# A causal depthwise convolution inside a hybrid decoder layer: 15 of its 62 tap operations move from VectorE to GpSimd

## The chip, the cores and the metric

One core of a Trainium2 chip. The metric is the device time of one launch in microseconds (us), the median of several executions. PE is TensorE (PEld its weight loads), DVE is VectorE, ACT is ScalarE, POOL is GpSimd, SP is SyncE, which here only issues DMAs.

## The reference, cut to what matters

One decoder layer for 512 prompt rows and 8 sample rows, width 1024. After one combined projection `z = x @ w_in`, four head groups work side by side (a convolution module, two kinds of sparse attention, a pooling mixer), then comes an output projection, a layer norm, a feed-forward block (1024 to 4096 to 1024) and a second layer norm. The change concerns the convolution module alone:

```python
def conv_module(u, buf, dw, dw_b, ln_g, ln_b, pw):
    a, g = jnp.split(u, 2, axis=-1)
    z = a * jax.nn.sigmoid(g)
    zc = jnp.concatenate([buf, z], axis=1)
    y = lax.conv_general_dilated(zc, dw[:, None, :], ...feature_group_count=C_CONV) + dw_b
    y = jax.nn.silu(layer_norm(y, ln_g, ln_b))
    return y @ pw, zc[:, -(CONV_W - 1):]
```

256 channels, each with a filter of 31 taps of its own over the rows before it, float32 throughout.

## The kernel before, in words

Channels lie on the 128 partitions and rows in the free dimension, so 256 convolution channels are two channel tiles, t = 0 and t = 1. One tap of one tile is one operation on 128 x 512 elements: `yc[t] += zc[t, k:k+512] * w[t, k]`, with the weight read from a column of `vec`. There are 31 x 2 = 62 of them, listed in `TAPS` in the order (k=0,t=0), (k=0,t=1), (k=1,t=0) and so on. All run on DVE (line 1299 for the two with k = 0, line 1302 for the other 60). Each waits on the semaphore `vtap` until the operation before the previous one has finished, since only that one wrote the same tile.

The program is written as one list of steps, `TL`, made by `timeline()`; each engine walks through this list and issues, in this order and in a queue of its own, what it has to do at each step. Nothing is reordered at run time, so a wait on an engine holds up everything behind it on that engine.

The first part of the list goes over the 18 panels of `w_in` (numbered 0 to 17; a panel is 1024 x 128 weights). For panel i:

- `load_panel`: SP loads it into one of three buffers `raw`.
- `split`: float32 products are made from three passes over rounded parts. ACT writes the rounded weights `wH` (line 941), DVE the rest `wL = raw - wH` (line 1240). `split i+1` stands ahead of `mm i` in the list.
- `mm`: PE runs 48 matmuls (line 597) and waits before them for `l_done`, the semaphore of `wL`.
- `evac`: ACT copies the sum out of PSUM into `zT`.

Between the panels other steps are strung, one stage of each per panel: `nsa b` for the eight sample sequences (PE: compression matmuls of line 606 and selection scores of line 623; DVE: lines 1258, 1264, 1268 and 1272, and at `kv` line 1275; ACT: lines 972 to 978), the `qn` copies (DVE, lines 1282 and 1283), and the convolution:

- after panel 4, `glu` (DVE, lines 1290 to 1293) writes `zc` and counts `glu_done` to 2;
- after each of the panels 4 to 9 a `taps` step, with 6, 6, 13, 13, 12 and 12 tap operations. In the list a `taps` step stands ahead of the `split` of the next panel but one: the taps after panel 7 stand ahead of `split 9`, which `mm 9` waits for;
- at the end of the last `taps` step the eight sample rows (lines 1307 to 1309) and `conv_done`;
- after panel 10 `cmean` (PE, line 750, waits for `conv_done`; DVE subtracts the mean, line 1354), later `cvar` and `cpw`, the norm and the pointwise product.

POOL has little to do: seven memsets at the start (line 1152), then `pdiff 0` after panel 8 and `pdiff 1` after panel 10 (running sums for the pooling mixer, lines 1164 to 1189, on the buffers `pa` and `pb`; `pdiff 0` waits for the last pooling panel, number 8, and its result is read by the PE step `pool 0`, line 738, after `cmean`, and waited for by SP ahead of the output of `pool_sample`), then one scaling per attention unit (line 1195), the residual of the first layer norm (line 1199) and a square per panel of the up projection (line 1204).

Of the kernel before, what the change touches and what calls it, by code (L numbers as in the profile page):

```python
# [8 lines left out]
ALU = mybir.AluOpType  # L9
# [7 lines left out]
T, B = 512, 8  # L17
# [9 lines left out]
CW = 31  # L27
# [48 lines left out]
PAD = ("pad", 0)  # L76
PADS = (0, 0, 0, 0, 0)
PER_PANEL = 7
TAPS = [(k, t) for k in range(CW) for t in range(2)]


def timeline():

    tl = [("load_x", 0), ("load_panel", 1), ("load_small", 0), ("load_panel", 2), ("load_w1", 0)]
    tl += [("split", 0)]
    tl += [("xsplit", k) for k in range(KT)]

    def panel(i, mid=()):
        out = []

        if i + 1 < N_PANELS and i + 1 != OUT0:
            out.append(("split", i + 1))
        if i + NRAW < N_PANELS and (i >= OUT0 or i + NRAW < OUT0):
            out.append(("load_panel", i + NRAW))
        out.append(("mm", i))
        out += list(mid)
        out.append(("evac", i))
        return out

    def spread(first, n, extras):  # L100

        out = []
        for q in range(n):
            out.append(("att", first + q))
            out += [s for s in extras[q * len(extras) // n:(q + 1) * len(extras) // n] if s != PAD]
        return out

    def pieces(i, first, n, extras):

        out = [s for s in panel(i) if s[0] not in ("mm", "evac")]  # L110
        q = 0
        for s in spread(first, n, extras):
            if s[0] == "att":
                out.append(("mm", i, q, n))
                q += 1
            out.append(s)
        return out + [("evac", i)]

    nt = 2 * CW
    taps = [0, nt // 10, nt // 5, nt // 5 + 13, nt // 5 + 26, nt // 5 + 38, nt]  # L120
    pending = []
    att = 0
    M = lambda lo, hi: [s for u in range(lo, hi) for s in (("mu", u), ("mp", u - 1))]
    extras = {15: M(1, 2) + [("ctr", 0), ("zrow", 0)] + M(2, 3) + [("cimp", 0)],
              16: M(3, 4) + [("zrow", 1)] + M(4, 7),
              17: M(7, 11)}
    for i in range(N_IN_PANELS):
        b = i - NSA_PANEL
        if i >= ATT_PANEL:
            tl += pieces(i, att, PER_PANEL, extras[i])  # L130
            att += PER_PANEL
        else:
            tl += panel(i, pending)
        pending = []
        if i == 1:
            tl.append(("load_nsa", 0))
        if i == 2:
            tl.append(("load_state", 0))
            tl.append(("cmpp", 0))
            pending = [("kv", 0)]  # L140
        if i == NSA_PANEL:
            tl.append(("qn", 0))
        if 0 <= b < B:
            tl.append(("nsa", b))
            pending = [("kv", b + 1)]
            if b < B - 1:
                tl.append(("load_nsa", b + 1))
        if b == B - 1:
            tl.append(("load_post", 0))
        if i == 4:  # L150
            tl.append(("glu", 0))
        if 4 <= i < 10:
            tl.append(("taps", (taps[i - 4], taps[i - 3])))
        if i == 8:
            tl += [("out_early", 0), ("pdiff", 0)]
        if i == 10:
            tl += [("cmean", 0), ("pool", 0), ("pdiff", 1), ("qm", 0), ("out_conv", 0)]
        if i == 11:
            tl += [("cvar", 0)]
        if i == 12:  # L160
            tl += [("cpw", 0), ("pool", 1), ("load_lo", 0)]
        if i == 14:
            tl += [("csc", 0), ("zcols", 0), ("win", 0), ("mu", 0)]
    tl += [("out_z", 0)]
    side = [("zrow", 2), ("own", 0), ("vrow", 0), ("vrow", 1), ("msplit", 0), ("msplit", 1), ("msplit", 2), ("msplit", 3)]
    for u in range(11, MU + 1):
        side += [("mu", u), ("selv", u - 11), ("mp", u - 1)]
    side += [("selv", k) for k in range(MU + 1 - 11, 4 * (B - 1))]
    side += [("stat", k) for k in range(3)] + [PAD] * PADS[0] + [("comb", 0)] + [PAD] * PADS[1] + [("comb", 1)] + [PAD] * PADS[2] + [("back", 0)] + [PAD] * PADS[3]
    for b in range(B + 1):  # L170
        side += [PAD] * PADS[4] + [("spv", b)] + ([("load_panel", OUT0 + b - 1)] if 1 <= b <= NRAW else [])
    side += [("split", OUT0), ("mpv", 0), ("fin", 0)]
    tl += spread(att, NU + LAG - att, side)
    tl += [("load_x", 1)]
    tl += [("msplit", q) for q in range(4, KT)]

    for i in range(OUT0, FF0):
        tl += panel(i, [("mean", 0, i - OUT0 - 1)] if i > OUT0 else [])
    tl += [("mean", 0, KT - 1), ("ln", 0)]
    for i in range(FF0, N_PANELS):  # L180
        k = i - (N_PANELS - KT)
        tl += panel(i, [("mean", 1, k - 1)] if k > 0 else [])
    tl += [("mean", 1, KT - 1), ("ln", 1)]
    return tl


TL = timeline()
# [51 lines left out]
def nth(bank, step):  # L239

    return USES[bank].index(step)


def build(nc, a, o):
    ctx = ExitStack()
    with ctx:
        def sem(name):
            return ctx.enter_context(nc.semaphore(name))
# [141 lines left out]
        h_done, l_done, mm_done = sem("h_done"), sem("l_done"), sem("mm_done")  # L390
        acc_read = [sem("acc_read_by_scalar"), sem("acc_read_by_vector")]
        const_done = sem("const_done")
        vch, ach, pch, vtap, vln = sem("vector_chain"), sem("scalar_chain"), sem("gpsimd_chain"), sem("tap_done"), sem("ln_scaled")
        bias_in = sem("bias_in")
        xc_done, cmp_mm, cmp_t1, cmp_u, cmp_th, hid_done, kv_mm, kc_done = (
# [745 lines left out]
        def _(pool):  # L1141
# [10 lines left out]
                nc.gpsimd.memset(buf, value).then_inc(const_done, 1)  # L1152
            up_no = 0
            for kind, n, *part in TL:
                if kind == "pdiff":

                    read(pool, ("mm", PANEL_SLOT.index(S_PO + 1)))
                    tt, copy = nc.gpsimd.tensor_tensor, nc.gpsimd.tensor_copy
                    x = zT[:, S_PO + n, :]
                    if n == 0:  # L1160
                        pool.wait_ge(small_in, 32)
                        pool.wait_ge(state_in, 32)
                        for t in range(2):
                            copy(sp[:, t, :, 15], zT[:, S_PO + t, T:NT])
                    else:
                        pool.wait_ge(pool_mm, 1)

                    def double(dst, src, w):
                        copy(dst[:, 0:w], src[:, 0:w])
                        chain(tt(dst[:, w:T], src[:, w:T], src[:, 0:T - w], ALU.add))  # L1170

                    double(pa, x, 1)
                    double(pb, pa, 2)
                    if n == 1:
                        double(pa, pb, 4)
                        double(pb, pa, 8)
                    w0, w1_ = ((2, 4), (8, 16))[n]

                    for lo, s in ((0, pa), (HD, pb)):
                        q = slice(lo, lo + HD)  # L1180
                        tt(pb[q, 0:16], s[q, 0:16], cst[q, C_INVC + 16 * n:C_INVC + 16 * n + 16], ALU.mult)
                        chain(nc.gpsimd.tensor_scalar(pb[q, 16:T], s[q, 16:T], cst[q, C_INVW + n:C_INVW + n + 1], None, ALU.mult))
                    for lo, w in ((0, w0), (HD, w1_)):
                        rows = slice(lo, lo + HD)
                        chain(copy(pb[rows, T:NT], sp[rows, n, :, 15]))
                        for k in range(1, w):
                            chain(tt(pb[rows, T:NT], pb[rows, T:NT], sp[rows, n, :, 15 - k], ALU.add))
                    chain(nc.gpsimd.tensor_scalar(pb[:, T:NT], pb[:, T:NT], cst[:, C_INVW + n:C_INVW + n + 1], None, ALU.mult))
                    tt(pb[:, :], pb[:, :], x, ALU.subtract).then_inc(pool_d, 1)
# [19 lines left out]
        def _(dve):  # L1209
# [22 lines left out]
            for step in TL:  # L1232
# [62 lines left out]
                elif kind == "taps":  # L1295
                    for k, t in TAPS[n[0]:n[1]]:
                        w = vec[:, V_DW + t * CW + k:V_DW + t * CW + k + 1]
                        if k == 0:
                            ts(yc[:, t, 0:T], zc[:, t, 0:T], w, vec[:, V_DWB + t:V_DWB + t + 1], ALU.mult, ALU.add).then_inc(vtap, 1)
                        else:  # L1300
                            dve.wait_ge(vtap, taps - 1)
                            stt(yc[:, t, 0:T], zc[:, t, k:k + T], w, yc[:, t, 0:T], ALU.mult, ALU.add).then_inc(vtap, 1)
                        taps += 1
                    if n[1] == len(TAPS):
                        tmp = Vn[:, 0, :, :].rearrange("p a b -> p (a b)")[:, 0:B * CW].rearrange("p (b k) -> p b k", b=B)
                        for t in range(2):
# [438 lines left out]
```

## Time and profile before

| | us |
|---|---|
| median of 3 runs | 944.61 (940.42 to 953.58) |
| the profiled execution, its own time | 934.16 |
| its span, first to last instruction | 932.4 |
| busy in the span: PE, DVE, ACT, POOL | 846.1, 435.2, 281.9, 143.9 |

The profile is one execution. Its span is what the rows below are measured in; 1.8 us lie around it. The stretch that the change touches runs from 43.5 us (`glu`) to about 115 us (`cmean`), one tenth of the span.

### The profile page before, as it was taken

The numbers are of one execution on the slowest core, as the hardware profiler recorded it, in microseconds if no ns is written. First come the engines' busy times: TensorE is split into PE (matmuls) and PEld (weight loads), VectorE is DVE, ScalarE is ACT, GpSimd is POOL, SyncE is SP. The second block draws the span as 40 slices with busy tenths as digits, with TensorE's granted clock in tenths as the row PEclk, the third lists the DMA queues.
The fourth block names the chain that finished last, engine by engine and source line by source line (L and its number), as shares of the span: only waits on it lengthen the run. The fifth ranks groups of instructions, "written<-read, shape, count | busy, mean of one in ns | idle before, by whom it ended". The sixth has DMA issues, their size and how long they took to land.

```text
span 932.4 us, 17901 instructions
## 1 busy us (share of the span) xinstructions
PE 846.1 (91%) x6901; PEld 733.2 (79%) x6901; DVE 435.2 (47%) x961; ACT 281.9 (30%) x610; POOL 143.9 (15%) x171
## 2 busy tenths in 40 slices
PE   6999899599899988689899499999999999999993
PEld 6988688466545554378798499999999999999992
DVE  3389953466655675541424633333333333333325
ACT  4222243243422343221312433331133113311104
POOL 0005350022221333111000611110011001100000
PEclk9999999799765899789999699999999999999997
DMA  9455743545646785112333023333323332233202
GB/s 324 132 161 157 191 137 114 204 136 182 211 152 182 225 256 146 32 46 90 96 90 137 1 91 91 91 91 92 94 87 91 101 97 77 94 108 91 68 1 92
DMA packets 73295, 113.26 MB, mean 121 GB/s; under 512 B 25177, under 2 KB 42202, under 8 KB 72538
## 3 DMA queue, kind: packets, MB, share of 16 engines
q1 hardware_dynamic: 65146, 110.28, 38.0%
q10 hardware_dynamic: 8064, 1.84, 0.9%
q8 instruction: 55, 0.90, 0.4%
q14 instruction: 30, 0.25, 0.1%
HBM read 107.66 MB, written 6.52 MB: 122 GB/s over the span
## 4 chain that ended last, share of the span: by engine, by line
PE 54%; DVE 3%; POOL 2%; ACT 1%; ACTq 1%; issue 1%; DVEq 0%
PE psum L597 44%; PE psum L858 2%; PE psum L900 2%; POOL xres L1199 2%; PE psum L909 1%; PE psum L843 1%; PE psum L671 1%; DVE std L1602 1%; PE psum L642 1%; ACT xres L1137 1%; PE psum L825 1%; PE psum L653 0%; PE psum L860 0%; ACTq L1011 0%; ACTq L1010 0%
## 5 line engine op out<-in xcount | busy, mean ns | idle before, releaser
L597 PE MATMUL psum<-opH,wH 128*128 128x260 f32 (+1 forms) x928 | 195.3, 292 | 27.6 <-DVE opL L1613 11.8
L597 PE MATMUL psum<-opH,wL 128*128 128x260 f32 (+1 forms) x928 | 190.2, 287 | 0.0
L597 PE MATMUL psum<-opL,wH 128*128 128x260 f32 (+1 forms) x928 | 189.9, 287 | 0.0
L597 PEld LDWEIGHTS psum<-opH,wH 128*128 128x128 f32 (+1 forms) x928 | 146.2, 192 | 39.1 <-issue 21.2
L941 ACT ACTIVATE wH<-raw 128x1024 fp32r<-128x1024 f32 x90 | 93.9, 1043 | 182.2 <-PE psum L597 178.3
L597 PEld LDWEIGHTS psum<-opH,wL 128*128 128x128 f32 (+1 forms) x928 | 145.5, 191 | 0.4
L597 PEld LDWEIGHTS psum<-opL,wH 128*128 128x128 f32 (+1 forms) x928 | 145.2, 191 | 0.4
L1240 DVE TENSOR_TENSOR wL<-raw,wH 128x1024 fp32r<-128x1024 f32 x90 | 109.1, 1212 | 51.3 <-ACT wH L941 51.3
L597 PE MATMUL psum<-hidH,wH 128*128 128x260 f32 x512 | 104.2, 285 | 0.0
L597 PE MATMUL psum<-hidH,wL 128*128 128x260 f32 x512 | 103.2, 283 | 0.0
L597 PE MATMUL psum<-hidL,wH 128*128 128x260 f32 x512 | 103.0, 283 | 0.0
L1195 POOL TENSOR_SCALAR PB<-PB,ps_small 128x31 f32<-128x31 f32 (+4 forms) x64 | 58.2, 909 | 235.7 <-DVE ps_small L1350 177.8
L1584 DVE TENSOR_TENSOR hidL<-hsq,hidH 128x520 fp32r<-128x520 f32 x32 | 22.4, 701 | 127.5 <-POOL hsq L1204 127.5
L597 PEld LDWEIGHTS psum<-hidH,wH 128*128 128x128 f32 x512 | 79.4, 188 | 0.4
L597 PEld LDWEIGHTS psum<-hidH,wL 128*128 128x128 f32 x512 | 78.9, 188 | 0.0
L597 PEld LDWEIGHTS psum<-hidL,wH 128*128 128x128 f32 x512 | 78.7, 188 | 0.0
L1592 DVE SCALAR_TENSOR_TENSOR xres<-xres,psum 128x520 f32<-128x520 f32 x32 | 22.3, 695 | 111.6 <-PE psum L597 111.6
L1204 POOL TENSOR_TENSOR hsq<-relu 128x520 f32<-128x520 f32 x32 | 33.8, 1055 | 242.4 <-ACT relu L1116 242.4
L1022 ACT ACTIVATE PB<-psum,ps_small 128x31 f32<-128x31 f32 (+4 forms) x64 | 29.9, 468 | 127.7 <-DVE ps_small L1333 79.8
L1116 ACT ACTIVATE relu<-psum 128x520 f32<-128x520 f32 x32 | 19.4, 605 | 117.2 <-PE psum L597 117.2
L642 PE MATMUL psum<-zT 64*128 64x128 f32 (+3 forms) x96 | 45.4, 557 | 0.0
L671 PE MATMUL psum<-PT,Vn 128*64 128x128 f32 x240 | 42.6, 316 | 0.0
(287 smaller groups left out, 997.9 us busy)
## 6 DMA issues: line engine op xcount, KB each, us to landing
raw<-in_panels SPq DMA_DIRECT2D x89, 512.0 KB, 3.6
moba_lo<-in_moba_pages SPq DMA_DIRECT2D x64, 256.0 KB, 3.4
moba_hi<-in_moba_pages SPq DMA_DIRECT2D x64, 256.0 KB, 3.7
nsa_ring<-in_nsa_pages SPq DMA_DIRECT2D x128, 96.0 KB, 2.2
selV<-in_selv_pages SPq DMA_DIRECT2D x72, 32.0 KB, 2.2
xres<-in_xT SPq DMA_DIRECT2D x8, 260.0 KB, 5.4
xres<-in_xT SPq DMA_DIRECT2D x1, 2080.0 KB, 8.8
out_y<-xres SPq DMA_DIRECT2D x8, 260.0 KB, 2.1
```

The lines of the kernel that those rows point to most:

```text
L597: last = mm(out[0:M, hf, 0:HALF], w, x[:, k, hf * HALF:(hf + 1) * HALF], start=(t == 0 and j == 0), stop=(t == KT - 1 and j == 2))
L642: mm(psum[:, 4 + u % 2, 0:n], q, k, start=True, stop=True).then_inc(qk_done, 1)
L671: last = mm(out, Vn[:, src, j, off:off + HD], PT[:, u % 2, j * P:(j + 1) * P], start=(FIRST[u] and j == 0), stop=(LAST[u] and j == i), ski ...
L858: mm(out, PTs[:, b % 2, p // 8, p % 8, :], V[:, p, :], start=False, stop=False, skip_group_check=True)
L941: fn(wH[:, n % NW].rearrange("p a b -> p (a b)")[:, 0:m], raw[:, n % NRAW, 0:m], ACT.Copy).then_inc(h_done, 1)
L1022: fn(PB[:, u % 2, 0:m], psum[:, 4 + u % 2, 0:m], ACT.Exp, bias=ps_small[:, u % 2:u % 2 + 1], accum_out=ps_small[:, 4 + u % 2:5 + u % 2]).t ...
L1116: fn(zview(relu[:, up_no % 2, :]), acc(("mm", n))[:, :, 0:HALF], ACT.Relu).then_inc(acc_read[0], 1)
L1195: nc.gpsimd.tensor_scalar(PB[:, u % 2, 0:m], PB[:, u % 2, 0:m], ps_small[:, 8 + u % 2:9 + u % 2], None, ALU.mult).then_inc(scaled, 1)
L1204: nc.gpsimd.tensor_tensor(hsq[:, up_no % 2, :], relu[:, up_no % 2, :], relu[:, up_no % 2, :], ALU.mult).then_inc(sq_done, 1)
L1240: tt(wL[:, n % NW].rearrange("p a b -> p (a b)")[:, 0:m], raw[:, n % NRAW, 0:m], wH[:, n % NW].rearrange("p a b -> p (a b)")[:, 0:m].bitca ...
L1584: tt(hidL[g % 2][:, m, :], hsq[:, up_no % 2, :], hidH[g % 2][:, m, :].bitcast(F32), ALU.subtract).then_inc(hid_l_done, 1)
L1592: stt(x, x, ALPHA if g == 0 else 1.0, acc(("mm", n))[:, :, 0:HALF], ALU.mult, ALU.add).then_inc(acc_read[1], 1)
```

## The change

The last 15 taps (k = 16 to 30) of tile t = 1 leave `TAPS`, which then has 47 entries: both tiles for k = 0 to 15, tile 0 alone for k = 16 to 30. The steps of `taps` are cut anew: 5, 5, 10, 11, 10 and 6 operations after the panels 4 to 9.

POOL gets the 15 taps as one block, at the first `taps` step of the list, as soon as `glu_done` is 2: one product into `pa`, then 14 times a product into `pb` and an addition `pa += pb`, 29 instructions, each of which waits for the one before it (the second product, into another buffer, waits for none). At the end of the fourth `taps` step (`TAP_CUT`, after panel 7 and ahead of `split 9`) DVE waits for all 29, adds `pa` to `yc` of tile 1 and waits for that addition. `pdiff 0`, which reuses `pa` and `pb`, waits for it too. In the wait of a DVE tap, the previous operation is now waited for where it wrote the same tile.

```diff
+POOL_TAPS = 15
+TAPS = [(k, t) for k in range(CW) for t in range(2) if t == 0 or k < CW - POOL_TAPS]
...
-    nt = 2 * CW
-    taps = [0, nt // 10, nt // 5, nt // 5 + 13, nt // 5 + 26, nt // 5 + 38, nt]
+    nt = len(TAPS)
+    taps = [0, nt // 9, 2 * nt // 9, 4 * nt // 9, 6 * nt // 9, 8 * nt // 9, nt]
...
+TAP_CUT = [s[1] for s in TL if s[0] == "taps"][3]
...
+                if kind == "taps" and n[0] == 0:
+                    pool.wait_ge(glu_done, 2)
+                    for q, k in enumerate(range(CW - POOL_TAPS, CW)):
+                        w = vec[:, V_DW + CW + k:V_DW + CW + k + 1]
+                        if q == 0:
+                            nc.gpsimd.tensor_scalar(pa[:, :], zc[:, 1, k:k + T], w, None, ALU.mult).then_inc(ptap, 1)
+                        else:
+                            if q > 1:
+                                pool.wait_ge(ptap, 2 * q - 1)
+                            nc.gpsimd.tensor_scalar(pb[:, 0:T], zc[:, 1, k:k + T], w, None, ALU.mult).then_inc(ptap, 1)
+                            pool.wait_ge(ptap, 2 * q)
+                            nc.gpsimd.tensor_tensor(pa[:, :], pa[:, :], pb[:, 0:T], ALU.add).then_inc(ptap, 1)
                 if kind == "pdiff":
...
                     if n == 0:
+                        pool.wait_ge(ptap_add, 1)
...
-                            dve.wait_ge(vtap, taps - 1)
+                            dve.wait_ge(vtap, taps - (TAPS[taps - 1][1] != t))
...
+                    if (n[0], n[1]) == TAP_CUT:
+                        dve.wait_ge(vtap, taps)
+                        dve.wait_ge(ptap, 2 * POOL_TAPS - 1)
+                        tt(yc[:, 1, 0:T], yc[:, 1, 0:T], pa[:, :], ALU.add).then_inc(ptap_add, 1)
+                        dve.wait_ge(ptap_add, 1)
```

## Rows read from the trace of the kernel before

**Rows 1.** The page: span, and busy tenths in 40 slices of 23.3 us
```profile
span 932.4 us, 17901 instructions
...
DVE  3389953466655675541424633333333333333325
...
POOL 0005350022221333111000611110011001100000
```

**Rows 2.** The timeline of PE, 43 to 115 us: start, length, instruction, [idle before]
```profile
49.93 0.47 PE L597 MATMUL psum<-opH,wH 128*128 128x260 f32 x2 [1.34 <-DVE wL L1240]
...
84.99 0.48 PE L597 MATMUL psum<-opH,wH 128*128 128x260 f32 x2 [1.18 <-DVE wL L1240]
...
97.62 0.48 PE L597 MATMUL psum<-opH,wH 128*128 128x260 f32 x2 [1.16 <-DVE wL L1240]
...
110.51 1.99 PE L750 MATMUL psum<-yc,mean 128*128 128x260 f32 x8 [1.40 <-DVE yc L1309]
...
114.65 0.41 PE L597 MATMUL psum<-opH,wH 128*12 128x260 f32 x2 [1.27 <-DVE yc L1354]
```

**Rows 3.** The timeline of DVE, 43 to 97 us
```profile
44.80 0.16 DVE L1293 SCALAR_TENSOR_TENSOR sc<-zT 128x8 f32<-128x8 f32 x1
...
75.01 8.70 DVE L1302 SCALAR_TENSOR_TENSOR yc<-zc,vec,yc 128x512 f32<-128x512 f32 x13
83.63 1.22 DVE L1240 TENSOR_TENSOR wL<-raw,wH 128x1024 fp32r<-128x1024 f32 x1
...
87.62 8.71 DVE L1302 SCALAR_TENSOR_TENSOR yc<-zc,vec,yc 128x512 f32<-128x512 f32 x12
```

**Rows 4.** Line 1302: its 60 taps, ns min/median/max
```profile
L1302 DVE SCALAR_TENSOR_TENSOR yc<-zc,vec,yc x60: 737/743/1084, 45.9 to 107.5; 128x512 f32<-128x512 f32 x60
```

**Rows 5.** Groups of POOL by shape: count, busy us, mean ns
```profile
L1204 POOL TENSOR_TENSOR hsq<-relu 128x520 f32<-128x520 f32 x32 | 33.8, 1055 | 242.4 <-ACT relu L1116 242.4
L1195 POOL TENSOR_SCALAR PB<-PB,ps_small 128x512 f32<-128x512 f32 x12 | 18.8, 1565 | 39.2 <-DVE ps_small L1344 22.0 <-DVE ps_small L1350 17.2
...
L1189 POOL TENSOR_TENSOR pb<-pb,zT 128x520 f32<-128x520 f32 x2 | 2.6, 1311 | 0.2
...
L1170 POOL TENSOR_TENSOR pa<-zT 128x511 f32<-128x511 f32 x2 | 2.1, 1036 | 0.0
```

**Rows 6.** The timeline of POOL, 80 to 122 us
```profile
80.02 5.01 POOL L1164 COPY sp<-zT 128x8 f32<-128x8 f32 x2 [77.91 <-ACT zT L958]
84.97 0.18 POOL L1169 COPY pa<-zT 128x1 f32<-128x1 f32 x1
85.19 1.03 POOL L1170 TENSOR_TENSOR pa<-zT 128x511 f32<-128x511 f32 x1
86.28 0.19 POOL L1169 COPY pb<-pa 128x2 f32<-128x2 f32 x1
...
87.77 2.59 POOL L1182 TENSOR_SCALAR pb<-pa,cst 64x496 f32<-64x496 f32 x1
...
93.82 0.59 POOL L1187 TENSOR_TENSOR pb<-pb,sp 64x8 f32<-64x8 f32 x1
...
119.99 1.52 POOL L1182 TENSOR_SCALAR pb<-pa,cst 64x496 f32<-64x496 f32 x1
```

**Rows 7.** The timeline of DVE at 89 us and 115 us, two single instructions
```profile
88.95 1.08 DVE L1302 SCALAR_TENSOR_TENSOR yc<-zc,vec,yc 128x512 f32<-128x512 f32 x1
...
114.91 1.05 DVE L1285 COPY QM<-zT 64x8 f32<-64x8 f32 x1
```

**Rows 8.** The waits of PE, 150 to 180 us: total, times, longest
```profile
PE psum L791 <- DMA winV<-in_winV: 6.2, 1, 6.2
```

**Rows 9.** Windows: busy us of PE, PEld, DVE, ACT, POOL, then granted clock
```profile
155.00:168.00 13.00, 10.61 (x97) 8.78 (x95) 6.05 (x13) 4.30 (x11) 0.00 (x0) 1.00 0.27 90
168.00:175.00 7.00, 2.68 (x52) 2.71 (x56) 0.00 (x0) 0.00 (x0) 0.00 (x0) 0.51 1.01 401
175.00:178.00 3.00, 1.46 (x39) 1.00 (x32) 2.33 (x4) 0.00 (x0) 0.00 (x0) 1.00 1.01 378
```

More of the change, by code:

```diff
@@ L78 @@
 PER_PANEL = 7
-TAPS = [(k, t) for k in range(CW) for t in range(2)]
+POOL_TAPS = 15
+TAPS = [(k, t) for k in range(CW) for t in range(2) if t == 0 or k < CW - POOL_TAPS]
+TAP_ADD = len(TAPS)
 def timeline():
@@ L392, in build @@
         const_done = sem("const_done")
+        ptap, ptap_add = sem("gpsimd_tap_done"), sem("gpsimd_taps_added")
         vch, ach, pch, vtap, vln = sem("vector_chain"), sem("scalar_chain"), sem("gpsimd_chain"), sem("tap_done"), sem("ln_scaled")
```

## The prediction

> **What bounds the kernel now.** The page first: over the whole span PE is busy 846 of 932 us, so what counts is where PE stands still. The slices of DVE [rows 1] show one stretch in which DVE and not PE is full: the slices from 47 to 117 us, with nines. Then the timeline of PE in this stretch [rows 2]: `mm 9` starts at 84.99 after an idle 1.18, `mm 10` at 97.62 after 1.16, `cmean` at 110.51 after 1.40, each released by DVE. A panel thus takes 97.62 - 84.99 = 12.63 us, of which PE works 12.63 - 1.16 = 11.47. The timeline of DVE [rows 3] shows the same period without a gap: `wL` at 83.63, the four microseconds of `nsa`, then 12 taps from 87.62 to the next `wL`. So in this stretch DVE is the bound, by little: with a DVE that is never late, PE would win its idle time: 1.34 + 1.18 + 1.16 + 1.40 and some tenths of the 1.27 at 114.65 [rows 2]; under 6 us in all. That is the most that any relief of DVE here can give.
>
> **What the change removes.** 15 taps. Thirteen taps take 8.70 us from start to end, less the overlap of two neighbours (the next instruction starts at 83.63, 8.62 after 75.01): 0.66 us each [rows 3], while one alone lasts 0.74 [rows 4]. 15 x 0.66 = 9.9 us of DVE.
>
> **What it adds on POOL.** 15 products and 14 additions, each behind the one before. A product on 128 x 512 with a weight from a column takes 1.565 us, twelve times over, [rows 5]. An addition of this size has two kinds of neighbours: 1.036 and 1.055 where both inputs are one tensor, 1.311 where they are two, in place, as here [rows 5]. I take 1.17, and keep 1.04 and 1.31. Between dependent POOL instructions lie 0.06 us (85.19 + 1.03 to 86.28) [rows 6]. Two more terms:
>
> The first real POOL instruction of the kernel is a copy of 128 x 8 at 80.02; with its like it takes 5.01, of which a small copy is 0.18 [rows 6]. About 4.7 us are thus paid once, before POOL first works. I take it that they move to the first product. Bounds: 0 and 4.7. (The Trainium skill, "GPSIMD Engine Reference", Instruction dispatch, has about 6 us for the first call of freshly loaded code; the row is of that kind, and I go by the row.)
>
> The second is contention. The product of line 1182 lasts 1.52 with DVE quiet at 119.99, but 2.59 at 87.77, with taps on DVE [rows 6]: 1.0 to 1.1 us lost, a tap and a half. An addition of 64 x 8 at 93.82 takes 0.59 where a small copy takes 0.19 [rows 6]: 0.35 to 0.4 lost, the rest of one tap. So a pair of product and addition takes 1.565 + 1.17 + 0.12 = 2.86 us alone, and about 2.86 + 1.05 + 0.37 = 4.3 beside taps. Before the cut DVE taps run in three stretches in which POOL already works, of some 3, 8 and 9 us. These hold five to six pairs (with what they themselves lengthen), and the first product. 6 x 1.42 + 1.05 = 9.6 us of waiting. Bounds: 5 us (POOL out of step with DVE) and 15 (additions that wait twice, as products do).
>
> POOL's last tap ends at: `glu` done 45.0 [rows 3] + 4.7 + 15 x 1.565 (23.5) + 14 x 1.17 (16.4) + 28 x 0.06 (1.7) + 9.6 = **100.9**.
>
> **What it adds on DVE.** While POOL is in, a tap is held up too: 1.08 in place of 0.74 [rows 7], and the 12 taps at 87.62 take 0.7 more than 12 x 0.66 for the two products they met [rows 3]. So 0.35 per product, and for an addition, which reads twice as much, between 0.35 and 0.9. Up to the cut DVE has 31 taps where it had 38, -4.6 us, and meets about seven pairs, +5 to +9. It comes to the cut at about 84 to 88, where before it came to `wL 9` at 83.63 [rows 3]. There it waits for POOL, 13 to 17 us. Queued behind the wait are `wL 9`, which `mm 9` needs, and then everything of DVE: PE runs out of work at about 85, after `nsa 2`. What happens to either engine before the cut no longer counts; POOL's chain is the path. The copies of `qn` may suffer too (a copy of 64 x 8 took 1.05 at 114.91 beside a POOL addition, [rows 7]), up to 4 us, all of it hidden by this wait.
>
> A rule speaks of this contention, and more strictly. The row shows a tap that loses 0.35 to a product of 2.59 us, most of which is therefore no lock [rows 6, 7]. The Trainium skill, "SBUF — State Buffer", Who interferes with whom, has DVE with two SBUF inputs and a reading POOL instruction exclude each other, an exclusive lock; taken for the whole instruction it makes the third rival below.
>
> **After the cut.** Add (0.1 + 0.65 + 0.1), `wL 9` 1.15, and 0.15 to the matmul: 2.1 us, so `mm 9` starts at 103.0 in place of 84.99: +18.0. From there:
>
> - The clock. PE's longest wait in the middle of the kernel, 6.2 us for `winV` [rows 8], was followed by seven microseconds at half the granted clock, 0.51, 1.2 in place of 2.4 GHz; then it was back; PE worked 2.7 of these seven [rows 9], which cost it half of that. Here PE stands 17 us, so I expect the same. The time at half speed after the restart I take as 4 us, a little more than those 2.7: +2.0 (bounds 0 and 4). The first panel then takes PE 11.47 + 2.0 = 13.5 where it took 12.63: +0.8. DVE would need 12.4: `wL` and `nsa` 4.0, and 10 taps, of which eight now wait for their predecessor in full, 0.74 + 0.04 [rows 4], 7.6, and about 0.9 for `pdiff 0` on POOL.
> - The second panel: DVE has 6 taps in place of 12, PE bounds at 11.47 where it took 12.89 (97.62 to 110.51): -1.4.
> - `cmean` to `mm 11`: DVE is no longer behind; of the 1.27 idle I give back 0.8. -0.8.
> - `pdiff 0` starts about 102 in place of 80 and without the 4.7 takes some 15 us: 117, and `pool 0` on PE comes after `cmean` at 128. Hidden, with 10 us to spare; so is SP's wait for it.
>
> Sum: 18.0 + 0.8 - 1.4 - 0.8 = **+16.6 us**. Nothing behind it gives this back: all the later steps hang on PE's order, and their loads are issued on semaphores that shift with it. On the profiled execution 934.2 + 16.6 = 950.8. The median of the runs shown is 10 us above this execution; 944.6 + 16.6 = **961**, 1.8% slower. A difference of 2%, 19 us, is about what a measurement of this kernel tells from none, so this lies just inside.
>
> **The rivals.** In short form, time change = (end of POOL's taps) - 86.3, and 2 more if the clock falls.
>
> - *POOL keeps up (not slower).* The 4.7 us don't move, an addition is 1.04, no waits: 45.0 + 23.5 + 14.6 + 1.7 = 84.8, DVE meets the cut without a wait, -1.5: 943. It decides if POOL ends before 86.3. For it: a short product is hardly longer than the row says. Against it: both the 5.01 and the 2.59 are in the trace. Chance 0.06.
> - *A cheaper chain.* No first call, or half the contention: POOL ends at 95 to 96, clock falls or not: +9 to +11, 954. Chance 0.24.
> - *The lock holds for the whole instruction.* Then DVE's two-input work between 50 us and the cut (21 taps and `wL 8`, 15 us) and POOL's run (91.3 without waits) stand one behind the other: 107, +22.5, 967. Against it the tap of 1.08. With an addition of 1.31 and two waits in each I get 105 by the softer way, +20.5. Chance of one or the other 0.20.
> - *The change doesn't do what it says*, i.e. the wait at the cut lets DVE go early: 29 counts are waited for and 29 given, so 0.01.
>
> **How the numbers follow.** The forecast has 0.49. Range: from 948 (POOL done at about 90, next to the first rival, which is left out) to 970 (the lock and a slow clock); this leaves out some 0.15 and takes in the scatter of the median, some 4 us. Slower by over 2%, POOL ending after 103.2 (or 105 with a full clock): the third rival and a third of the forecast's own width, 0.36. Faster by over 2% would need 19 us where 6 are to be had: 0.02. Within 2%: 0.62.
>
> **What would show it.** In the profile after: the first POOL product at 45 with about 7 us; POOL full from 45 to 101; products at 1.57 to 2.7; one DVE addition at line of the cut with an idle of 13 to 17 us before it, ended by POOL; one PE idle of about 17 us ahead of `mm 9`; granted clock 0.5 around 100; taps of 1.08 and more, and after the cut at 0.78 apart; no PE idle on DVE's account at `mm 10` and `cmean`. It is wrong if POOL ends by 88, if the idle at the cut is under 5 us, or if the bound after the cut is `pdiff 0`.

## The result, and the profile after

The changed kernel is slower: the ratio of its time to that of the kernel before is 1.0178, with a 95% interval from 1.0121 to 1.0235 (20 executions of each). On the 942.67 us median of the kernel before this is +16.8 us. The plain medians lie closer, 949.54 against 942.67, +6.9 us, because the ratio counts of each kernel only the executions within 1.5% of its fastest, 11 of 20 after and 6 of 20 before, and leaves out the slower ones. The profiled execution took 949.7 us with a span of 947.9, against 934.16 and 932.4.

Where does it go? A way to read this is to follow the start of each panel's first matmul in both traces. The third column is the difference, the fourth what each step adds:

```
panel   before    after    later by   added here
6        49.93    50.91      0.98       0.98  (lies before the first tap: the loads at the start)
7        60.43    63.37      2.94      +1.96
8        72.37    77.67      5.30      +2.36
9        84.99    99.28     14.29      +8.99
10       97.62   113.35     15.73      +1.44
11      114.65   128.21     13.56      -2.17
13      145.80   159.35     13.55       0
14      157.29   172.42     15.13      +1.58
40      614.28   629.86     15.58      +0.45
```

So of 15.6 us, 1.0 comes before the convolution starts (I count it as scatter: the traces of e1, e2 and e4 below have it too, whatever their edit), 12.6 in the stretch that the change touches and 2.0 behind it.

The slices of the page show the shape: POOL, which was idle from 2 to 80 us, is full from 46 to 99, and DVE's full stretch (the slices of 8 and 9) stays about as full [rows 1].

```profile
span 947.9 us, 17919 instructions
...
DVE  3398865266664566472332643333333332333325
...
POOL 0099751011221232311000341110011001100000
```

The timeline of PE, the rows that answer to those of before [rows 2]. The waits for `wL` ahead of panels 8 and 9 have grown (from 0.45 and 1.18 to 2.83 and 8.62), and a new one, for the copies of `qn`, has come in; the one at panel 6 is as it was (1.32); the waits at panel 10 and at `cmean` are gone, and the last one is down from 1.27 to 0.52:

```profile
62.37 0.62 PE L629 MATMUL psum<-nsa_ring,QNa 128*32 128x512 f32 x2 [1.88 <-DVE QNb L1303]
77.67 0.58 PE L603 MATMUL psum<-opH,wH 128*128 128x260 f32 x2 [2.83 <-DVE wL L1260]
99.28 0.77 PE L603 MATMUL psum<-opH,wH 128*128 128x260 f32 x2 [8.62 <-DVE wL L1260]
...
128.21 0.41 PE L603 MATMUL psum<-opH,wH 128*12 128x260 f32 x2 [0.52 <-DVE yc L1379]
```

The timeline of DVE [rows 3]. In brackets is the idle time before a row and who ended it:

```profile
46.00 1.29 DVE L1319 TENSOR_SCALAR yc<-zc,vec 128x512 f32<-128x512 f32 x2
...
65.39 10.99 DVE L1322 SCALAR_TENSOR_TENSOR yc<-zc,vec,yc 128x512 f32<-128x512 f32 x10
76.31 1.21 DVE L1260 TENSOR_TENSOR wL<-raw,wH 128x1024 fp32r<-128x1024 f32 x1
...
80.31 12.10 DVE L1322 SCALAR_TENSOR_TENSOR yc<-zc,vec,yc 128x512 f32<-128x512 f32 x11
97.19 0.69 DVE L1327 TENSOR_TENSOR yc<-yc,pa 128x512 f32<-128x512 f32 x1 [4.78 <-POOL pa L1173]
97.91 1.22 DVE L1260 TENSOR_TENSOR wL<-raw,wH 128x1024 fp32r<-128x1024 f32 x1
...
101.91 8.43 DVE L1322 SCALAR_TENSOR_TENSOR yc<-zc,vec,yc 128x512 f32<-128x512 f32 x10
```

What to see here: ten taps now take 11.0 us and eleven 12.1, 1.1 us each, where thirteen took 8.7 before. DVE reaches the cut at 92.4 and waits only 4.8 us for GpSimd. The larger part of DVE's loss is thus not a wait. It stands in the rows as work, as a longer tap. Three neighbouring taps, one by one:

```profile
67.75 1.77 DVE L1322 SCALAR_TENSOR_TENSOR yc<-zc,vec,yc 128x512 f32<-128x512 f32 x1
...
69.44 1.18 DVE L1322 SCALAR_TENSOR_TENSOR yc<-zc,vec,yc 128x512 f32<-128x512 f32 x1
...
70.54 0.74 DVE L1322 SCALAR_TENSOR_TENSOR yc<-zc,vec,yc 128x512 f32<-128x512 f32 x1
```

and what POOL did beside them:

```profile
46.06 1.84 POOL L1167 TENSOR_SCALAR pa<-zc,vec 128x512 f32<-128x512 f32 x1 [43.96 <-DVE sc L1313]
...
67.58 1.39 POOL L1173 TENSOR_TENSOR pa<-pa,pb 128x512 f32<-128x512 f32 x1
69.07 1.88 POOL L1171 TENSOR_SCALAR pb<-zc,vec 128x512 f32<-128x512 f32 x1
71.04 1.37 POOL L1173 TENSOR_TENSOR pa<-pa,pb 128x512 f32<-128x512 f32 x1
...
94.18 1.56 POOL L1171 TENSOR_SCALAR pb<-zc,vec 128x512 f32<-128x512 f32 x1
95.82 1.26 POOL L1173 TENSOR_TENSOR pa<-pa,pb 128x512 f32<-128x512 f32 x1
98.01 1.31 POOL L1184 COPY sp<-zT 128x8 f32<-128x8 f32 x2 [0.93 <-DVE yc L1327]
```

The two engines fall into step. A tap that begins with an addition of POOL lasts 1.77, 1.03 more than one that meets nothing; one that meets a product lasts 1.18, 0.44 more; a third goes free. One round, product and addition of POOL against three taps of DVE, takes 69.07 to 72.50, 3.4 us, where the three taps alone took 2.0. The last two rows of the chain, with DVE quiet, are the prices without contention: 1.56 and 1.26.

The windows around the wait (busy us of PE, PEld, DVE, ACT, POOL, then the granted clock) show the second price of a stall. The granted clock is at half speed from 95.0, while PE stands still, to 105.2, six microseconds after it has started again: 0.54 in the middle window, against 1.00 on both sides. (A shorter fall, from 77.9 to 81.3, follows the wait of 2.83 ahead of panel 8; DVE is behind there, so PE only waits less for the next `wL`.)

```profile
84.00:95.00 11.00, 6.66 (x54) 5.26 (x53) 8.40 (x8) 1.41 (x5) 10.46 (x7) 1.00 0.38 103
95.00:106.00 11.00, 6.72 (x34) 6.75 (x35) 8.60 (x13) 1.89 (x3) 9.69 (x12) 0.54 0.40 111
106.00:113.00 7.00, 7.00 (x61) 6.01 (x59) 5.91 (x8) 1.40 (x5) 6.37 (x9) 1.00 0.62 138
```

### The profile page after: what moved, and what is told of

It is laid out like the page before. It is cut to its first block, busy times and chain, and to the rows that moved or that the text cites. A ratio compares the mean times of both kernels' runs of the same rounds, so it can differ in the third digit from the quotient of the medians.

```text
span 947.9 us, 17919 instructions
## 1 busy us (share of the span) xinstructions
PE 851.2 (90%) x6901; PEld 738.8 (78%) x6901; DVE 444.6 (47%) x947; ACT 281.1 (30%) x610; POOL 187.8 (20%) x200
## 3 DMA queue, kind: packets, MB, share of 16 engines
q10 hardware_dynamic: 8064, 1.84, 0.9%
## 4 chain that ended last, share of the span: by engine, by line
PE 53%; DVE 3%; POOL 2%; ACT 1%; ACTq 1%; issue 0%; DVEq 0%
PE psum L603 44%; PE psum L864 2%; PE psum L906 2%; POOL xres L1219 2%; PE psum L915 1%; PE psum L849 1%; PE psum L677 1%; DVE std L1627 1%; PE psum L648 1%; ACT xres L1143 1%; PE psum L831 1%; PE psum L659 0%; PE psum L866 0%; ACTq L1017 0%; ACTq L1016 0%
## 5 line engine op out<-in xcount | busy, mean ns | idle before, releaser
L603 PE MATMUL psum<-opH,wH 128*128 128x260 f32 (+1 forms) x928 | 198.0, 296 | 35.7 <-DVE wL L1260 12.8
L603 PE MATMUL psum<-opH,wL 128*128 128x260 f32 (+1 forms) x928 | 192.7, 290 | 0.0
L603 PE MATMUL psum<-opL,wH 128*128 128x260 f32 (+1 forms) x928 | 192.6, 290 | 0.0
L603 PEld LDWEIGHTS psum<-opH,wH 128*128 128x128 f32 (+1 forms) x928 | 148.8, 195 | 47.1 <-issue 29.9
L603 PEld LDWEIGHTS psum<-opH,wL 128*128 128x128 f32 (+1 forms) x928 | 148.2, 195 | 0.4
L603 PEld LDWEIGHTS psum<-opL,wH 128*128 128x128 f32 (+1 forms) x928 | 148.0, 195 | 0.4
L1322 DVE SCALAR_TENSOR_TENSOR yc<-zc,vec,yc 128x512 f32<-128x512 f32 x45 | 44.5, 1033 | 0.5
```

The costliest lines, as they stand in the source:

```text
L603: last = mm(out[0:M, hf, 0:HALF], w, x[:, k, hf * HALF:(hf + 1) * HALF], start=(t == 0 and j == 0), stop=(t == KT - 1 and j == 2))
```

## Experiments

After the result two theories stood against each other. *Chain*: as in my prediction, GpSimd's 29 instructions are too long, and the wait at the cut is the loss. *Contention*: the two engines hold each other up where they work side by side, and DVE loses more by it than the 15 taps were worth. All times in this table are from the first tap on DVE, in us, read from the traces. e2, e3, e4, e9 and e10 were executed once each (955.02, 965.85, 929.39, 972.36 and 946.53 us, at mean clocks from 0.901 to 0.945), so that only their stretch is read and not their time:

```
                     panel 7    8      9     10     11     12     14    panel 15
before                 15.4   27.4   40.0   52.6   69.7   82.6  112.3   132.7
changed                17.4   31.7   53.3   67.3   82.2   95.1  126.4   147.2
e1 taps gone           14.8   26.2   37.6   49.4   64.2   77.1  106.9   128.2
e2 pool extra          19.4   36.9   54.9   68.5   84.9   97.8  127.5   147.9
e3 memset chain        17.1   30.1   50.4   63.9   78.8   91.7  123.0   144.4
e5 cut later           17.4   31.7   47.7   61.2   76.0   89.0  120.3   141.9
e6 eight taps          19.1   32.9   45.7   58.6   73.4   86.4  116.1   137.5
e8 taps spread         15.4   26.9   38.3   49.7   61.2   78.0  110.8   136.0
e9 products only       15.5   27.4   54.8   68.3   83.2   96.2  127.5   148.7
e10 additions only     22.7   44.0   57.9   69.4   84.2   97.2  126.9   147.7
```

**e1: what is there to win?**

```diff
-                if kind == "taps" and n[0] == 0:
-                    pool.wait_ge(glu_done, 2)
...
-                    if (n[0], n[1]) == TAP_CUT:
-                        dve.wait_ge(vtap, taps)
...
```

> The changed kernel with GpSimd's 15 taps left out altogether (this part of the convolution is missing from the output), no addition, no wait at the cut; VectorE has its 47 taps. What counts is the start of panels 9 and 11 on TensorE, from VectorE's first tap (before: 40.0 and 69.7 us after it; changed: 53.3 and 82.2). If all of the loss comes from GpSimd's work, by its length or by contention, both lie below the kernel before: panel 9 at 38 to 39, panel 11 at 64 to 65, since TensorE then bounds; the span about 5 us under before. This is also the ceiling of any unloading of VectorE here. If instead the new cutting of the taps steps or the longer wait between taps of one tile costs something, panel 11 stays at 67 or more.

Panel 9 at 37.6, panel 11 at 64.2: PE bounds, and neither the new cutting of the steps nor the longer wait costs it anything. With the taps gone for nothing, the stretch is 5.5 us shorter. That is all that any unloading of DVE can bring here; my prediction had "under 6". Yet this kernel's time was not seen to be lower: ratio 1.0114, interval 0.9995 to 1.0233, from four executions. Its profiled execution is 4.4 us ahead of the kernel before at panel 14 (157.29 to 152.91 in the spans' own time) and 17 us behind at panel 17. Nothing of the program differs there; the granted clock does, as these windows of the two traces show, e1 first, then the kernel before:

```profile
163.00:250.00 87.00, 77.17 (x474) 51.38 (x474) 35.54 (x133) 19.16 (x75) 8.57 (x15) 0.52 0.37 127
```

```profile
163.00:250.00 87.00, 71.71 (x670) 48.81 (x668) 51.41 (x194) 29.03 (x113) 13.42 (x22) 0.92 0.56 184
```

So one execution says little about 5 us, and I read the stretch by its panels from here on.

**e2: contention without a wait.** The kernel before, all 62 taps on VectorE, and in it:

```diff
+                if kind == "taps" and n[0] == 0:
+                    pool.wait_ge(glu_done, 2)
...
                     if n == 0:
+                        pool.wait_ge(ptap, 29)
```

> The kernel before with all 62 taps on VectorE, plus the 29 GpSimd instructions of the change as extra work whose result nobody reads (only the pooling step behind them on GpSimd waits). No wait of VectorE for GpSimd, so what is lost is contention alone. Contention theory: where both engines are at work, three taps take 3.45 us and not 2.0, for each product and addition; some 12 of the 14 pairs meet taps, so VectorE loses 15 to 18 us until GpSimd's end, and panel 9 starts at 40.0 + 13 to 16 = 53 to 56 us after the first tap, as late as in the changed kernel though nobody waits. Chain theory (my prediction's step: only the wait at the cut counts, and a pair costs VectorE 0.7 to 1.25): panel 9 at 40.0 + 5 to 9 = 45 to 49.

Panel 9 at 54.9: the contention theory, and not the chain. The timeline of DVE in this kernel, where no instruction waits for GpSimd; thirteen taps, 8.7 us before, take 14:

```profile
67.14 14.51 DVE L1317 SCALAR_TENSOR_TENSOR yc<-zc,vec,yc 128x512 f32<-128x512 f32 x13
...
85.56 14.10 DVE L1317 SCALAR_TENSOR_TENSOR yc<-zc,vec,yc 128x512 f32<-128x512 f32 x13
```

GpSimd's work beside the taps costs here as much as the whole change does, with no tap waiting for its result. This kernel keeps all 62 taps on DVE, though, so that more of them meet GpSimd; what contention costs with the 15 taps gone, e5 shows.

**e3: the chain without reading.**

```diff
-                    for q, k in enumerate(range(CW - POOL_TAPS, CW)):
...
+                    for q in range(NFILL):
+                        if q:
+                            pool.wait_ge(ptap, q)
+                        nc.gpsimd.memset(pa[:, :], 0.0).then_inc(ptap, 1)
```

> The changed kernel with GpSimd's 29 instructions replaced by 82 memsets of the same buffer, each waiting for the one before, about 51 us in all; these write and read nothing (15 taps are missing from the output). The length of GpSimd's chain stays, the reading goes. VectorE should run its taps 0.66 apart again and come to the cut about 33 to 36 us after its first tap, then wait 15 us or more for GpSimd. Chain theory: panel 9 starts at 53 us as in the changed kernel, since GpSimd ends at the same time. If contention by itself carried the loss, panel 9 would come much earlier, which the wait for the 82 memsets rules out unless they are shorter than 0.6 us each; so the thing to read is the split: tap spacing 0.66 against 1.15, wait at the cut 15 against 4.8.

```profile
56.91 0.48 DVE L1297 COPY QNa<-zT 64x8 f32<-64x8 f32 x1 [2.38 <-ACT zT L953]
57.40 0.57 DVE L1298 COPY QNb<-zT 64x8 f32<-64x8 f32 x1
...
64.19 6.71 DVE L1317 SCALAR_TENSOR_TENSOR yc<-zc,vec,yc 128x512 f32<-128x512 f32 x10
...
77.45 7.37 DVE L1317 SCALAR_TENSOR_TENSOR yc<-zc,vec,yc 128x512 f32<-128x512 f32 x11
93.65 0.69 DVE L1322 TENSOR_TENSOR yc<-yc,pa 128x512 f32<-128x512 f32 x1 [8.83 <-POOL pa L1168]
```

The taps are 0.66 apart again: what holds a tap up is not that GpSimd is busy or writes, which memsets do too; what they lack is reading. DVE comes to the cut 39.4 us after the first tap (not 33 to 36: PE bounds the steps before it, and the copies of `qn` take 0.57 and not 0.17 beside memsets) and waits 8.8 for a chain of 48.1, less than the 15 or more that I expected. Panel 9 is at 50.4, late by the length of the chain. The length was chosen near the 51 that the chain has beside taps, so it holds what the taps cost GpSimd. Alone, products and additions would need 15 x 1.56 + 14 x 1.26 + 28 x 0.09 = 43.6, and panel 9 would come at about 46 (an estimate from these rows and from the 2.2 us between the end of the chain and panel 9). So both theories hold by themselves, and neither gives the whole: the chain as long as it was gives 50.4, contention without a wait gives 47.7 (e5 below), the two together 53.3 against 40.0 before. This is less than both shifts added, as time that contention takes from DVE is time that it would otherwise have waited.

**e4: what were the 4.9 us of POOL's first copy?**

```diff
+            nc.gpsimd.tensor_copy(pa[:, 0:8], mean1024[:, 0:8]).then_inc(early, 1)
+            pool.wait_ge(early, 1)
+            nc.gpsimd.tensor_copy(pa[:, 0:8], mean1024[:, 0:8]).then_inc(early, 1)
+            pool.wait_ge(early, 2)
             up_no = 0
             for kind, n, *part in TL:
```

> The kernel before with two copies of 128 x 8 on GpSimd at its very start, when VectorE is idle. If GpSimd's first real instruction pays about 4.7 us once, the first of the two takes about 4.9 us and the copy of the pooling step, at about 80 us, then takes 0.2 to 1.0. If instead the 4.9 us of that copy were a wait for VectorE's taps, both early copies take about 0.2 and the one at 80 us still 4.9. No effect on the span either way.

```profile
2.16 0.19 POOL L1155 COPY pa<-mean 128x8 f32<-128x8 f32 x1
2.41 0.19 POOL L1157 COPY pa<-mean 128x8 f32<-128x8 f32 x1
...
81.05 4.94 POOL L1170 COPY sp<-zT 128x8 f32<-128x8 f32 x2 [78.44 <-ACT zT L959]
```

The first real instruction costs 0.19, and the copy at 81 us is as long as ever. It is no price of a first call. What keeps it out shows in e1, where the same copy starts at 79.95 and takes 2.97: there the stretch of taps and the `wL` behind it end at 82.7, and the copy at 82.9; in the kernel before they end at 84.85, and the copy at 85.0. So the copy waits for the end of DVE's stretch. Why this copy was kept out over six taps, while small copies at 94 us got in after one, no run here shows.

**e5: the cut one step later.**

```diff
-TAP_CUT = [s[1] for s in TL if s[0] == "taps"][3]
+TAP_CUT = [s[1] for s in TL if s[0] == "taps"][4]
```

> The changed kernel with the addition of GpSimd's sum one taps step later, after panel 8, ahead of split 10 (index 4 for 3 in TAP_CUT). VectorE has 10 more taps before it must wait, 8 us or so, and came to the old cut 4.8 us before GpSimd was done. The wait goes. Times from the first tap (changed: panel 9 at 53.3, panel 11 at 82.2; before: 40.0 and 69.7): panel 9 at 47 to 49, panel 11 at 76 to 78. If the wait were the loss, as my prediction had it, panel 11 would come to about 70, level with the kernel before; by contention 6 to 8 us stay. The pooling step, which waits for the addition, then starts 61 us after the first tap and may be 1 us late for its matmul.

Panel 9 at 47.7 and panel 11 at 76.0. The wait has gone, its row has no idle time any more, and 6.2 of the 12.5 us at panel 11 with it; 6.3 are left, which is what contention costs beyond what the 15 taps were worth. The pooling step was not late. (One of the ten executions took 1993.85 us and is not used.) Against the kernel before, the ratio is 1.0024, interval 0.9953 to 1.0094.

```profile
96.25 8.74 DVE L1322 SCALAR_TENSOR_TENSOR yc<-zc,vec,yc 128x512 f32<-128x512 f32 x10
105.02 0.69 DVE L1327 TENSOR_TENSOR yc<-yc,pa 128x512 f32<-128x512 f32 x1
```

**e6: eight taps.**

```diff
-POOL_TAPS = 15
+POOL_TAPS = 8
```

> The changed kernel with 8 taps on GpSimd instead of 15 (54 on VectorE, steps of 6, 6, 12, 12, 12, 6). GpSimd's chain is 26 to 27 us and ends long before the cut, so no wait there. Contention theory: a pair still costs VectorE 1.45 us and saves it 0.66, so the half-sized change still loses: panel 9 at 42 to 45 us after the first tap (before 40.0), panel 11 at 70 to 72 (before 69.7). If a short chain were harmless, VectorE would have 8 taps less, 5 us: panel 9 at 38.5, panel 11 at 66.

Panel 9 at 45.7 and panel 11 at 73.4, 0.7 and 1.4 us beyond my range: also a chain of 27 us, that nobody waits for, costs more than 8 taps are worth. A part of what was missing is at the start: with 6 taps in the first step and contention on them, `wL` comes late for panel 6 already (6.7 us after the first tap, before 4.9). Against the kernel before, the ratio is 1.0137, interval 1.0039 to 1.0236, from four executions.

**e9 and e10: which of the two instructions is it?**

```diff
-  nc.gpsimd.tensor_tensor(pa[:, :], pa[:, :], pb[:, 0:T], ALU.add).then_inc(ptap, 1)
+  nc.gpsimd.tensor_scalar(pa[:, :], zc[:, 1, k:k + T], w, None, ALU.mult).then_inc(ptap, 1)
```

for e9, and for e10, from the third product on:

```diff
-  nc.gpsimd.tensor_scalar(pb[:, 0:T], zc[:, 1, k:k + T], w, None, ALU.mult).then_inc(ptap, 1)
+  nc.gpsimd.tensor_tensor(pa[:, :], pa[:, :], pb[:, 0:T], ALU.add).then_inc(ptap, 1)
```

> The changed kernel with each of GpSimd's 14 additions replaced by a second product of the same kind (15 taps are then missing from the output's sum): 29 products in a chain. In the changed kernel a tap that meets a product lasts 1.18 us instead of 0.74, one that meets an addition 1.77. If it is the reading that excludes (one input stream for a product, two for an addition), taps beside products alone are never over about 1.2 us, and about one tap in two or three is held up: the 10 taps of the third stretch take 8 to 9 us instead of 11.0. If every GpSimd instruction held the tap for most of its length, 1.56 us each, the 10 taps would take 12 or more.

```profile
64.28 8.36 DVE L1322 SCALAR_TENSOR_TENSOR yc<-zc,vec,yc 128x512 f32<-128x512 f32 x10
...
99.22 0.69 DVE L1327 TENSOR_TENSOR yc<-yc,pa 128x512 f32<-128x512 f32 x1 [13.12 <-POOL pa L1173]
```

> The changed kernel with GpSimd's products, all but the first two, replaced by additions of the same kind (15 taps are then missing from the output's sum): 2 products and 27 additions in a chain. By the same reading theory every addition holds one tap up by about 1.03 us, and one addition and its gap take about 1.4 to 1.5 beside taps: in 2 us of VectorE 2 taps at most, the 10 taps of the third stretch take 12 to 15 us. GpSimd's chain is 27 x 1.45 + 4 = 43 us at most and ends before the cut, so VectorE hardly waits there, though panel 9 is still late by contention, 48 to 52 us after the first tap.

```profile
71.07 16.95 DVE L1325 SCALAR_TENSOR_TENSOR yc<-zc,vec,yc 128x512 f32<-128x512 f32 x10
...
101.54 0.69 DVE L1330 TENSOR_TENSOR yc<-yc,pa 128x512 f32<-128x512 f32 x1
```

Ten taps take 8.4 us beside products, no tap over 1.18, and 17.0 beside additions, more than the 12 to 15 that I gave it: every tap meets one. A product is the longer instruction (1.56 against 1.26 alone) and the cheaper neighbour. It reads one stream of 512, an addition two, and a tap is held for 0.44 and 1.03. Whether it is the number of streams that counts, or something else in which the two instructions differ, no run here separates. In e9 DVE waits 13.1 us at the cut; this comes near the kernel that my prediction described, with a wait of 13 to 17, though its chain ends 52.6 us after the first tap and not 55.9. e10 missed its expectation twice more: its chain ended 47.7 us after the first tap, not within 43, and panel 9 came at 57.9, not at 48 to 52, later than in any other run, with no wait at the cut.

**e8: the same relief without GpSimd.** All 62 taps on DVE, in seven steps; the steps behind the convolution one panel later.

```diff
-    taps = [0, nt // 10, nt // 5, nt // 5 + 13, nt // 5 + 26, nt // 5 + 38, nt]
+    taps = [0, 6, 12, 22, 32, 42, 52, nt]
...
-        if 4 <= i < 10:
+        if 4 <= i < 11:
...
-        if i == 10:
+        if i == 11:
             tl += [("cmean", 0), ("pool", 0), ("pdiff", 1), ("qm", 0), ("out_conv", 0)]
-        if i == 11:
+        if i == 12:
             tl += [("cvar", 0)]
-        if i == 12:
+        if i == 13:
             tl += [("cpw", 0), ("pool", 1), ("load_lo", 0)]
```

> The kernel before without any GpSimd taps: all 62 taps on VectorE, over seven steps (6, 6, 10, 10, 10, 10, 10) after panels 4 to 10, and cmean, the pooling steps and out_conv after panel 11, cvar after 12, cpw and load_lo after 13, each one panel later. VectorE's idle time after panel 10 is used, so TensorE should bound: panel 9 at 38.5 to 39.5 us after the first tap, panel 11 at about 62 (no cmean before it), panel 12 at 77 to 78 (before 82.6), panel 14 at 107 to 108 (before 112.3). This is the 5 us that the change was after, without contention, unless load_lo, now later, makes TensorE wait for its pages at the first attention units; then up to 5 us come back by panel 15 (before 132.7).

Panel 12 comes at 78.0 in place of 82.6, as expected; at panel 14 only 1.5 of these 4.6 us are left, and at panel 15 it is 3.3 us behind in this execution, partly by the clock (half speed from 165.6 to 186.1; before from 168.1 to 175.0 and from 181.8 to 185.2), partly by a wait before the first attention unit, 5.8 us where the kernel before has 1.5:

```profile
PE psum L791 <- DMA winV<-in_winV: 5.9, 1, 5.9
PE psum L804 <- issue: 5.8, 1, 5.8
```

The first matmul of line 804 reads `moba_lo`. Its loads, 4.3 us of issuing on SP's queue, start at 170.15, behind those of `winK`, `winV` and `moba_hi`; in the kernel before they started at 146.78. The kernel before first, then e8:

```profile
146.78 4.31 SPq L451 DMA_DIRECT2D moba_lo<-in_moba_pages  x8
```

```profile
170.15 4.29 SPq L451 DMA_DIRECT2D moba_lo<-in_moba_pages  x8
180.32 1.08 PE L804 MATMUL psum<-moba_lo,QM 128*32 128x128 f32 x16 [5.80 <-issue]
```

The last piece of the first loads lands at 180.23, and the matmul starts at 180.32. So the later `load_lo` makes PE wait, as the expectation feared; the 5.8 us are this wait and not the clock. Its ratio is 1.0021, interval 0.9964 to 1.0078: no difference that can be measured. A version with `load_lo` left where it was, I did not try.

**A reading across all executions.** Every execution comes with its span and its mean granted clock. For the 44 executions of six kernels that the ratios rest on (those of the kernel before are taken from the experiments' comparisons) I fitted one line: span = own constant + slope x (1 - clock) x span. The slope is 0.65, and what remains scatters by 2.1 us, where the spans themselves run from 919 to 952. The constants, against the kernel before, with 95% bounds:

```
changed          +9.4 +- 2.1     (mean clock 0.938; before 0.950)
e5 cut later     +2.9 +- 2.4
e6 eight taps    +4.5 +- 3.6
e1 taps gone     -4.1 +- 3.7
e8 taps spread   -2.7 +- 2.0
```

In this measure the order is that of panel 11, but for e5 and e6, which stand the other way round and within each other's bounds. The changed kernel's own steps cost 9.4 us, and the rest of its 16.8 comes as granted clock: some of it surely by its stall, as the window at 95 us shows; how much of the lower mean of the whole span is the change's doing and how much chance, the runs don't settle.

## Why the prediction was right

The forecast was +16.6 us, 1.8%, just inside 2%; measured are 1.78% and, in the trace, +15.6. Its direction, its size and its mechanism in the large (GpSimd too slow, DVE not relieved, PE starved of `wL 9`, a clock that falls) hold. The time itself did less well: 961 was forecast and 949.54 measured, 1.5 above the low end of the range, as the plain medians lie only 6.9 apart. Several steps of the sum do not hold, and that it came within 1 us is in part luck: errors of both signs met in it.

- *What bounds; what can be won.* Right. Under 6 us were said, e1 shows 5.5.
- *The product, 1.565 us.* Right: 1.56. *The addition, 1.17*: measured 1.26, between the bounds; +1.3 us over 14. *Gaps of 0.06*: 0.08 to 0.1, +1.
- *The 4.7 us of a first instruction.* Wrong, by misreading one row. The copy of 5.01 stood beside a stretch of taps, and I took for a one-off price what was contention, a term that I had in the sum already. The first product in the changed kernel takes 1.84, and e4 shows 0.19 for a first copy. The page that I named beside it, the Trainium skill's "GPSIMD Engine Reference", Instruction dispatch, speaks of freshly loaded code; no copy, product or addition here shows such a price.
- *Waits of POOL, 9.6 us.* Measured: 51.0 of chain (46.06 to 97.08) less 15 x 1.565, 14 x 1.26 and 28 x 0.09 leave 7.4. The chain was to end 55.9 us after the first tap and ended after 51.1: 4.8 less. The 4.7 that were not there make this up, as the other three terms (+1.3, +0.8 and -2.2) cancel.
- *What DVE loses, 0.35 per product and 0.35 to 0.9 per addition.* This is the step that failed most. An addition holds a tap for 1.03, outside my bounds, a product for 0.44, and more of them met taps than the seven pairs I counted, eight additions and ten products: the 29 taps of line 1322 ahead of the cut take 31.6 us in place of 19.1, +12.5 where I had +5 to +9. DVE came to the cut at 92.4 and not at 84 to 88, and waited 4.8 us, not 13 to 17. By my own sign of being wrong, an idle at the cut of under 5 us, the mechanism as I told it was wrong here: up to the cut DVE was nearly as late as POOL, and taking away the wait alone (e5) gives back only 6.2 of 12.5 us. For the forecast it made no difference, as POOL still ended last: with DVE early, it would have waited instead, as in e3.
- *The rule of the lock.* The row had 0.35 for a product, and I set the lock for the whole instruction aside for both kinds. For a product that was right: a tap is held 0.44 by an instruction of 1.56, and the tap of 69.44 ends at 70.62, before the product that it met (69.07 to 70.95). That the two do contend is what the Trainium skill, "SBUF — State Buffer", Who interferes with whom, states; its exclusive lock, taken for the whole instruction, the product does not bear out. For an addition it comes close: 1.03 of 1.26.
- *The `qn` copies, up to 4 us, hidden.* They took 4.2 where they took 1.5, and made PE wait 1.88; hidden behind panel 9, as said.
- *After the cut.* `mm 9` came 53.3 us after the first tap (forecast 58.0, before 40.0). The clock fell from 95.0 to 105.2, so the panel after the restart took 14.07 (forecast 13.5). The next two steps gave back 2.17 (forecast 2.2). `pdiff 0` ended at 113 and was hidden.
- *Nothing behind it.* There came 2.0 us more behind panel 13, while the clock was low for 3.4 us at 160 us, where it was not before. I had no term for it. In sum: 4.7 less at `mm 9`, 0.6 more in the panel after it, 2.0 behind and 1.0 at the start make 15.5 of 16.6. The last two, 3.0 us for which the prediction had no term, are what brought the sum back to the forecast.

## What to carry over

Before moving elementwise work from VectorE to GpSimd, look in the trace for the two side by side and price the neighbour, not only the mover: here a GpSimd instruction that reads two streams costs VectorE 1.03 us, more than the 0.66 of the tap that it was to save. So GpSimd's taps beside VectorE's lose, as 15 and 8 of them did; GpSimd's taps in a stretch in which VectorE runs none were not tried. A contention like this shows in no table of waits; it shows as instructions that last longer. Compare the mean and the maximum of one line: the median of the taps only went from 743 to 752 ns, as half of them met nothing long, but the maximum went from 1084 to 1775. And count how much idle time of the bounding engine there is to win before anything else: it was 5.5 us of 932, less than the granted clock moves one execution.

## What the runs showed of the hardware

- VectorE with two SBUF inputs beside GpSimd (128 x 512, float32): held 0.44 us by a product with one input stream, 1.03 by an addition with two, not at all by memsets (e3). GpSimd in turn waits 0.3 us (product, 1.56 to 1.88) and 0.1 (addition, 1.26 to 1.37) once the two are in step, product and addition in turn; with products alone it is 0.1 (1.66, e9), with additions alone 0.3 (1.60, e10).
- Small VectorE copies of 64 x 8 are held by memsets too: 0.57 in place of 0.17 (e3). Beside additions every second one takes 1.15, and a `wL` 2.29 in place of 1.21 (e10).
- A GpSimd copy of 128 x 8 came through only at the end of a stretch of VectorE taps and the `wL` behind it: 5.01 for it and its like in the kernel before, 2.97 in e1, where the stretch ended 2.1 us earlier.
- GpSimd's product, one input, is slower than its addition, two inputs: 1.56 against 1.26; with both inputs from one tensor an addition takes 1.04 [rows 5].
- PE stood still for the 8.6 us before 99.28; the granted clock was 0.50, 1.2 in place of 2.4 GHz, from 95.0 to 105.2.
- The kernel before spans 919.3 us at a mean granted clock of 0.957 and 932.4 at 0.936.
